# Attention of a two-layer hybrid transformer with expert retrieval: MLA heads one at a time in two of the six tiles

## The reference, cut to what matters

```python
def softmax_attend(q, k, v):                      # 8 MLA heads
    s = jnp.einsum('bqhd,bkhd->bhqk', q, k).astype(jnp.float32) * (q.shape[-1] ** -0.5)
    p = jax.nn.softmax(s, axis=-1)
    return jnp.einsum('bhqk,bkhd->bqhd', p.astype(v.dtype), v)

def diff_attend(q, k, v, lam):                    # 4 differential heads
    s = jnp.einsum('bqhcd,bkhcd->bhcqk', q, k).astype(jnp.float32) * (q.shape[-1] ** -0.5)
    p = jax.nn.softmax(s, axis=-1)
    a = p[:, :, 0] - lam * p[:, :, 1]
    return jnp.einsum('bhqk,bkhd->bqhd', a.astype(v.dtype), v)
```

## Time and profile before

| | us |
|---|---|
| median of 3 runs | 2632.14 (2626.13 to 2635.8) |
| the profiled execution | 2623.53 |
| its span | 2621.6 |
| TensorE busy | 2067.3 (79%) |
| VectorE busy | 1832.3 (70%) |
| ScalarE busy | 1119.5 (43%) |
| GpSimd busy | 975.2 (37%) |
| data moved | 980.25 MB, mean 374 GB/s |

### The profile page before, as it was taken

One profiled execution on the slowest core, in us unless ns is written; L12 is line 12 of the kernel. 1 busy time (PEld: TensorE's weight loads), 2 busy tenths in 40 slices (PEclk: granted clock), 3 DMA queues, 4 the chain that ended last, 5 costly groups with the idle time before them and its releaser, 6 DMA issues.

```text
span 2621.6 us, 26027 instructions
## 1 busy us (share of the span) xinstructions
PE 2067.3 (79%) x6888; PEld 1088.7 (42%) x6888; DVE 1832.3 (70%) x4176; ACT 1119.5 (43%) x3090; POOL 975.2 (37%) x916
## 2 busy tenths in 40 slices
PE   6997787777979876988677797878867988577766
PEld 2554444443435444444334343435543444333322
DVE  0147986995567779976979665644597787767776
ACT  2123474444236443744443723432244644333333
POOL 1012343332443433444343444320133443445453
PEclk8998898888998988989889898998988998888888
DMA  8588999997999999999999999994799999999997
GB/s 342 172 301 321 405 395 402 404 381 279 415 399 363 390 394 387 409 407 411 413 417 392 397 417 415 393 383 159 273 411 363 397 398 408 374 387 419 422 413 328
DMA packets 215704, 980.25 MB, mean 374 GB/s; under 512 B 17660, under 2 KB 75544, under 8 KB 117272
## 3 DMA queue, kind: packets, MB, share of 16 engines
q0 software_dynamic: 123648, 855.69, 80.1%
q1 hardware_dynamic: 91928, 123.05, 13.6%
HBM read 977.62 MB, written 1.05 MB: 373 GB/s over the span
## 4 chain that ended last, share of the span: by engine, by line
PE 32%; DVE 27%; DMA 22%; ACT 10%; issue 8%; POOL 1%; SPq 0%; POOLq 0%; DVEq 0%; ACTq 0%
DMA EXPERT<-in_peer_uv,FIX 19%; PE VS L1010 12%; PE PA L863 9%; DVE EXPERT L1630 9%; DVE ACC L1640 3%; DVE SCR L1264 2%; PE PA L891 2%; DMA WT<-in_peer_wq 2%; PE PB L787 2%; PE PB L1000 1%; PE VS L816 1%; ACT L1203 1%; PE PA L940 1%; PE PB L931 1%; ACT DIAG L1218 1%
## 5 line engine op out<-in xcount | busy, mean ns | idle before, releaser
L1010 PE MATMUL VS<-EXPERT,DIAG 128*128 128x512 f32 x2304 | 1170.4, 650 | 262.5 <-ACT DIAG L1218 261.8
L695 POOL DMA_INDIRECT EXPERT<-in_peer_uv,FIX x768 | 898.2, 1170 | 1088.4 <-PE VS L1010 739.1
L1630 DVE CUSTOM_DVE_ANT_0 EXPERT<-EXPERT,H 128x1024 f32<-128x1024 f32 x768 | 924.1, 1223 | 333.2 <-DMA EXPERT<-in_peer_uv,FIX 324.3
L1010 PEld LDWEIGHTS VS<-EXPERT,DIAG 128*128 128x128 f32 x2304 | 457.2, 209 | 840.9 <-issue 471.3
L1211 ACT ACTIVATE GEL<-DOT 128x1 f32<-128x1 f32 x768 | 155.2, 202 | 1046.6 <-DVE DOT L1630 1045.5
L863 PE MATMUL PA<-WT,HT 128*128 128x512 f32 (+2 forms) x720 | 294.5, 555 | 8.7 <-issue 5.4
L1640 DVE SCALAR_TENSOR_TENSOR ACC<-EXPERT,WEI,ACC 128x1024 f32<-128x1024 f32 x192 | 246.0, 1281 | 19.1 <-ACT WEI L1213 19.1
L1218 ACT ACTIVATE DIAG<-IDN,WEI 128x128 f32<-128x128 f32 x576 | 231.3, 402 | 60.0 <-PE VS L1010 41.9
L1000 PE MATMUL PB<-HT,WT 128*128 128x128 f32 (+1 forms) x1472 | 215.1, 308 | 35.1 <-issue 33.9
L1213 ACT ACTIVATE WEI<-GEL,GATE 128x1 f32<-128x1 f32 x768 | 226.3, 295 | 24.9
L1000 PEld LDWEIGHTS PB<-HT,WT 128*128 128x128 f32 x1472 | 207.8, 218 | 59.8 <-issue 57.2
(11 more groups left out here) (147 smaller groups left out, 1677.0 us busy)
## 6 DMA issues: line engine op xcount, KB each, us to landing
EXPERT<-in_w_ada POOLq DMA_DIRECT2D x48, 1024.0 KB, 11.9
WT<-in_peer_wq SPq DMA_DIRECT2D x92, 512.0 KB, 18.0
WT<-in_w_in SPq DMA_DIRECT2D x48, 512.0 KB, 10.0
WT<-in_w_out SPq DMA_DIRECT2D x48, 512.0 KB, 9.9
EXPERT<-in_peer_uv,FIX POOLq DMA_INDIRECT x768, 11.4
WT<-in_w_in SPq DMA_DIRECT2D x16, 384.0 KB, 9.8
WT<-in_w_in SPq DMA_DIRECT2D x16, 288.0 KB, 6.6
WT<-in_mla_wq_up SPq DMA_DIRECT2D x4, 512.0 KB, 10.0
```

Of the source, the lines that this page charges most:

```text
L695: pool.indirect_dma_start(out=EXPERT[:, j, :], out_offset=None, in_=a["peer_uv"], in_offset=bass.IndirectOffsetOnAxis(ap=FIX[:, par, j:j + ...
L1010: ins = nc.tensor.matmul(VSUM[n][:, :], DIAG[:, i, :], EXPERT[:, j, D + n * W:D + (n + 1) * W], start=first, stop=last_one)
L1630: nc.vector.tensor_tensor_reduce(out=EXPERT[:, j, 0:D], in0=EXPERT[:, j, 0:D], in1=H2[:, b % HB, :], scale=1.0, scalar=0.0, op0=ALU.mult, ...
```

## The change

The pairs of heads were in all six tiles. The change adds a function `units` that gives each tile its list of units: in `(0, CTX, 0)` and `(1, LAT, 0)` eight single MLA heads and four differential heads, 12 units in stages -1 to 13; in the other four tiles the same 4 pairs and 4 differential heads as before. An attention stage costs the planner 35 in the two tiles and 50 in the others, as before. In the opening the new number of stages and their cost change where `mingle` puts the products. The stage `gates` (one VectorE instruction) is put after stage 9 instead of stage 3 in the pause.

```diff
+def units(l, g, t):
+    size = 1 if (l, g, t) in ((0, CTX, 0), (1, LAT, 0)) else 2
+    return [("mla", tuple(range(h, h + size))) for h in range(0, MH, size)] + [("diff", (h,)) for h in range(DH)]
...
 def cost(s):
+    if s[0] == "attn":
+        return 50 if len(units(*s[1:4])) < MH + DH else 35
...
-    keys, attend, leave = front(1, LAT, (1,), queries=False), gates_early(attention(1, LAT, 0), 5), outward(1, LAT, (0,))
+    keys, attend, leave = front(1, LAT, (1,), queries=False), gates_early(attention(1, LAT, 0), MH + 3), outward(1, LAT, (0,))
...
# TensorE
-                if i + 1 < UNITS:
-                    u = i + 1
-                    for c in range(2):
+                todo = units(l, g, t)
+                if i + 1 < len(todo):
+                    kind, hs = todo[i + 1]
+                    for c in range(2 if kind == "diff" else len(hs)):
                         bank = fill_b()
...
-                    for c in range(2 if u < PAIRS else 1):
+                    for c in range(len(hs)):
                         bank = fill_a()
-                        turn_tiles(bank, [PR[:, u % 2, c, k * P:(k + 1) * P] for k in range(keys // P)], P)\
+                        turn_tiles(bank, [PR[:, (i - 1) % 2, c, k * P:(k + 1) * P] for k in range(keys // P)], P)\
...
# VectorE
-                    if done < PAIRS:
-                        tt(o.rearrange("p (c n) -> p c n", c=2), bank[:, 0:P].rearrange("p (c n) -> p c n", c=2),
-                           INV[:, done % 2, :].unsqueeze(2).to_broadcast([P, 2, MD]), ALU.mult).then_inc(emptied_a, 1)
+                    if done == "mla":
+                        tt(O[:, hs[0] * MD:hs[0] * MD + n].rearrange("p (c n) -> p c n", c=len(hs)),
+                           bank[:, 0:n].rearrange("p (c n) -> p c n", c=len(hs)),
+                           INV[:, i % 2, 0:len(hs)].unsqueeze(2).to_broadcast([P, len(hs), MD]), ALU.mult)\
+                            .then_inc(emptied_a, 1)
```

More of the change, by code:

```diff
@@ L106, in front @@
     return out
+def units(l, g, t):
+    size = 1 if (l, g, t) in ((0, CTX, 0), (1, LAT, 0)) else 2
+    return [("mla", tuple(range(h, h + size))) for h in range(0, MH, size)] + [("diff", (h,)) for h in range(DH)]
 def attention(l, g, t):
-    out = [("attn", l, g, t, i) for i in range(-1, UNITS + 2)]
+    out = [("attn", l, g, t, i) for i in range(-1, len(units(l, g, t)) + 2)]
     return out + [("gates", l, g, t), ("hnorm", l, g, t), ("rows", l, g, t, 0), ("heads", l, g, t), ("rows", l, g, t, 1)]
@@ L326, in make_plan @@
     plan += keys[:1] + g1 + [("adae", 1, 2)] + keys[1:at] + sh2[:2] + [("adat", 1, 2)] + keys[at:]
[L327 removed]
+    at = attend.index(("attn", 1, LAT, 0, MH + DH - 2)) + 1
     plan += attend[:at] + [sh2[2], attend[at], sh2[3], ("adae", 1, 3), attend[at + 1], sc2[0], attend[at + 2], ("adat", 1, 3)]
@@ L921, in attn @@
                     pe.wait_ge(emptied_a, ra.n)
-                if i + 1 < UNITS:
-                    u = i + 1
-                    for c in range(2):
+                todo = units(l, g, t)
+                if i + 1 < len(todo):
+                    kind, hs = todo[i + 1]
+                    for c in range(2 if kind == "diff" else len(hs)):
                         bank = fill_b()
-                        if u < PAIRS:
-                            q, k = QTM[:, 2 * u + c, t * P:(t + 1) * P], KTM[:, 2 * u + c, 0:keys]
-                        else:
-                            q = QTD[64 * c:64 * c + 64, u - PAIRS, t * P:(t + 1) * P]
-                            k = KTD[64 * c:64 * c + 64, u - PAIRS, 0:keys]
+                        if kind == "mla":
+                            q, k = QTM[:, hs[c], t * P:(t + 1) * P], KTM[:, hs[c], 0:keys]
+                        else:
+                            q = QTD[64 * c:64 * c + 64, hs[0], t * P:(t + 1) * P]
+                            k = KTD[64 * c:64 * c + 64, hs[0], 0:keys]
@@ L939, in attn @@
+                    for c, h in enumerate(hs):
                         for k in range(keys // P):
-                            last = nc.tensor.matmul(bank[:, c * MD:c * MD + n], PT[:, c, k * P:(k + 1) * P], v[:, k, at:at + n],
-                                                    start=(k == 0), stop=(k == keys // P - 1))
+                            last = nc.tensor.matmul(bank[:, c * n:(c + 1) * n], PT[:, c, k * P:(k + 1) * P],
+                                                    v[:, k, h * n:(h + 1) * n], start=(k == 0), stop=(k == keys // P - 1))
@@ L942, in attn @@
                     last.then_inc(filled_a, 1)
-                if 1 <= i <= UNITS:
-                    u = i - 1
-                    if u < PAIRS:
+                if 1 <= i <= len(todo):
+                    kind, hs = todo[i - 1]
+                    if kind == "mla":
                         pe.wait_ge(exp_ready, tick.so_far("units") + 1)
@@ L1151, in attn @@
                 keys = 2 * P if g == CTX else 4 * P
-                u = i + 1
+                u, todo = i + 1, units(l, g, t)
                 if u == 0 and t == 0 and l == g:
                     table_of(ACT.Exp)
-                if u < UNITS:
+                if u < len(todo):
+                    kind, hs = todo[u]
                     act.wait_ge(negmax_ready, tick("negmax"))
-                    for c in range(2):
+                    for c in range(2 if kind == "diff" else len(hs)):
                         bank = from_b()
                         ins = nc.scalar.activation(PR[:, u % 2, c, 0:keys], bank[:, 0:keys], ACT.Exp,
-                                                   bias=NM[:, u % 2, c:c + 1], scale=SC_M if u < PAIRS else SC_D,
+                                                   bias=NM[:, u % 2, c:c + 1], scale=SC_M if kind == "mla" else SC_D,
                                                    accum_out=SUM[:, u % 2, c:c + 1])
@@ L1459, in attn @@
                 keys = 2 * P if g == CTX else 4 * P
-                u = i + 1
-                if u < UNITS:
-                    for c in range(2):
+                u, todo = i + 1, units(l, g, t)
+                if u < len(todo):
+                    kind, hs = todo[u]
+                    maps = 2 if kind == "diff" else len(hs)
+                    for c in range(maps):
                         bank, n = rb.next()
@@ L1468, in attn @@
                 if i >= 2:
-                    done = i - 2
+                    done, hs = todo[i - 2]
                     bank = from_a()
-                    o = O[:, done * P:(done + 1) * P]
-                    if done < PAIRS:
-                        tt(o.rearrange("p (c n) -> p c n", c=2), bank[:, 0:P].rearrange("p (c n) -> p c n", c=2),
-                           INV[:, done % 2, :].unsqueeze(2).to_broadcast([P, 2, MD]), ALU.mult).then_inc(emptied_a, 1)
-                    else:
-                        nc.vector.tensor_copy(o, bank[:, 0:P]).then_inc(emptied_a, 1)
@@ L1477, in attn @@
-                if 1 <= i <= UNITS:
-                    for c in range(2 if i - 1 < PAIRS else 1):
+                    n = len(hs) * MD
+                    if done == "mla":
[3 more added lines that the diff above has]
+                            .then_inc(emptied_a, 1)
+                    else:
+                        at = MH * MD + hs[0] * P
+                        nc.vector.tensor_copy(O[:, at:at + P], bank[:, 0:P]).then_inc(emptied_a, 1)
@@ L1479, in attn @@
+                if 1 <= i <= len(todo):
+                    for c in range(len(todo[i - 1][1])):
                         bank = from_a()
                         nc.vector.tensor_copy(PT[:, c, 0:keys], bank[:, 0:keys]).then_inc(emptied_a, 1)
-                if u < UNITS:
+                if u < len(todo):
                     dve.wait_ge(dve_step, steps[0])
-                    nc.vector.tensor_scalar(NM[:, u % 2, :], MX[:, u % 2, :], -(SC_M if u < PAIRS else SC_D), None,
+                    nc.vector.tensor_scalar(NM[:, u % 2, 0:maps], MX[:, u % 2, 0:maps], -(SC_M if kind == "mla" else SC_D), None,
@@ L1484, in attn @@
                                             ALU.mult).then_inc(negmax_ready, 1)
-                if 0 <= i < UNITS:
+                if 0 <= i < len(todo):
+                    kind, hs = todo[i]
+                    maps = 2 if kind == "diff" else len(hs)
                     dve.wait_ge(exp_ready, tick("exp"))
                     dve.wait_ge(emptied_a, ra.n)
-                    link(nc.vector.reciprocal(INV[:, i % 2, :], SUM[:, i % 2, :]))
-                    if i >= PAIRS:
+                    link(nc.vector.reciprocal(INV[:, i % 2, 0:maps], SUM[:, i % 2, 0:maps]))
+                    if kind == "diff":
```

8 lines of the change are left out of this document (2 added, 6 removed).

## The result

| | us |
|---|---|
| median before | 2630.67 (5 runs, 2626.13 to 2635.8) |
| median with the change | 2616.1 (5 runs, 2603.73 to 2619.78) |
| ratio | 0.9948, 95% interval 0.9926 to 0.997 |
| the profiled execution | 2613.29, span 2611.3 |

14.6 us less, where 2.3 were forecast; the time lies just under the range. The page of the profile: busy times within 4 us of those before (weight loads 8.5 less), 24 VectorE instructions more.

A forecast was written before the change was run, and what follows sets the result against it. TensorE was taken as the bound in the opening's and the pause's attention, with gains only in its idle and slow time. Pause -2.9 and opening +0.6 gave -2.3 us, so 2632.1 became 2629.8 us; range 2617 to 2639.

The forecast's parts named there:

- The slow clock: Pause, 1811 to 1827 us: mean clock 0.62, about 12 us at 1.2 GHz; the forecast sum counted no gain from it.
- the other case: Rival that the slow clock goes too: pause gains 2.9 + 6 us, opening up to 3 more; chance 0.27.
- The long wait of the opening: TensorE's 2.45 us wait at the opening's first turn, right before clock 0.61 over 8 us; removed, with 2.5 at the second.
- Its size: Loss to the slow clock in the pause: half of about 12 us at 1.2 GHz, 6 us.
- the rival on the slow clock: Slow clock goes in the pause and perhaps the opening: kernel at 2620.8 to 2624 us; chance 0.27.
- Waits removed, start, more steps: Pause's attention: -4.0 us of waits, +0.35 at the start, +0.8 for steps; sum -2.9, ends -4.3 to -0.9.
- more steps: Pause: four more TensorE steps, 0.2 us each for switches between kinds of matmuls, +0.8 us (0 to 1.6).
- VectorE keeps up: Pause: TensorE stays the bound of a 2.46 us step by a tenth of a microsecond; extra small VectorE instructions cost nothing.
- The opening: Opening's attention: -2.45 us at the first turn, +2.5 at the second, +0.6 for steps; sum +0.6, from -2.4 to +2.
- Faster by over 0.5%: Whole kernel: both slow stretches gone and all waits with them, -13 us; chance 0.06.

The follow-up runs named there:

- run 4: Kernel before (pairs), with an idle 128x256 product ahead of each of the six waiting scores of the pause: 2617.96 us, ratio 0.9955 to before.
- run 9: Changed kernel, plus second scores of the pause's differential heads behind the transposes and the opening's second turn a stage later: 2613.55 us, ratio 0.996 to before.
- run 5: Changed kernel, with the pause's scores of heads 3, 5 and 7 made to wait for the preceding head's exponential: 2629.68 us, ratio 1.0011 to before.
- Run 10: Kernel of run 5, with two idle 128x256 products ahead of each of the three waits put back: 2620.14 us, ratio 0.9983 to before.
- run 3: Kernel before (pairs), with each unit's second score in the pause behind the transposes and its maximum behind the copies: 2608.34 us, ratio 0.9932 to before.
- run 6: Kernel of run 3, with the first turn of the opening one attention stage later: 2605.44 us, ratio 0.9918 to before.
- run 8: Changed kernel measured again, nothing altered, on another chip than the first follow-ups: 2615.67 us, ratio 0.9969 to before.
- run 1: Kernel before, with single heads in the pause tile alone and pairs kept in the opening: 2610.89 us, ratio 0.994 to before.
- run 12: Kernel before, unchanged, traced a second time: pause's attention 55.2 us at mean clock 0.72; no median given.

## Why the prediction was wrong

- *The slow clock*. This is the step that failed. The forecast left the 12 us at 1.2 GHz of the pause where they were and gave the other case 0.27. They hung on the waits: with these filled (run 4), and with most of them taken away by single heads (three traces) or late scores (four), the stretch ran at 1.00 throughout (run 9, which has both, fell for 3.4 us), with three waits put back (run 5) at 0.62. Run 10, filled in part, lies between. The rows had hinted at it: the fall came after 24 us with 5 us of idle time. I held against it that no row shows how small a gap is small enough, which is a reason for doubt about the size, not for leaving the clock as it was. What makes the clock fall at one gap and not at another stays open (1.47 us in run 3 without a fall, 0.86 in run 9 with one). The long wait of the opening, which the prediction set beside this one, is at least not needed for the slow stretch there: run 6 took it away and the stretch stayed, behind a wait of 0.68 us.
- *Its size*. The prediction priced it at 6 us from one execution; against run 4's 44.1 us, pairs at full clock, that execution gives 49.3 - 44.1 = 5.2, the other two traces 55.2 - 44.1 = 11.1. With the mean of the three (53.2) the pause gives 53.2 - 39.7 = 13.5 us; the medians gave 14.6, 17 and, in run 8, 7. The range ended at 2617 since it rested on the mildest execution, and the rival on the slow clock, 2620.8 at best with the opening's stretch in it, fell short of the measured 2616.1 too, though only the pause's stretch went.
- *Waits removed, start, more steps* (-2.9 us). The direction and the places were right; the size was 4.4: run 4, pairs at full clock with their waits, takes 44.1 us, and single heads 39.7. The term mis-sized is "more steps", +0.8: the step came out at 2.39 us and not 2.46, and half of a pair's step without its wait is 2.35 (from 1796.04 to 1801.86 us before, less 1.13), so the switches between kinds of matmuls cost next to nothing over what the pairs paid. The prediction left two waits, 0.55 and 0.61 us; three of 0.62 stand there. The third, at the last differential head, did not show before because the clock was slow there; run 4 has it too.
- *VectorE keeps up.* Right, with the small margin that was counted. The small instructions do cost VectorE time (busy 30.1 us instead of 28.8 in the stretch, for 12 more instructions) and cost the tile next to none, as the sum said.
- *The opening* (+0.6). Right, as far as it can be told: +0.5 in the mean of five executions each, with a spread of up to 3 us, and the wait moved to the second turn.
- *Faster by over 0.5%* got 0.06, and only with both slow stretches and all waits gone. One stretch and most of the waits of the pause were enough for 0.5% (0.6% in run 1, 0.3% in run 8). It should have been several times that.

## What to carry to other kernels

A short wait of TensorE can cost twice: its own length, and what its work loses if the clock falls for it. Here 4 to 5 us of waits, none over 1.13 us, brought 5 to 11 us more. Where a stretch at 1.2 GHz follows a row of gaps, count it as likely that it goes with them, but test it: in the opening it stayed when the long gap went. Trace more than one execution, since the length of such a stretch varies. Before splitting the work into smaller units, try to move the instruction that waits behind others that don't: that took all but one of these waits away from full-sized pairs, and though the transposes then waited 3.0 us for VectorE, the pause took 38.0 us in four traces, less than with single heads (39.6 to 39.8).

## What the runs showed of the hardware

The clock fell though no gap was longer than 1.13 us (pairs in the pause, three traces), and 1.4 us after the end of one of 1.89 us (run 5); it stayed up behind one of 1.47 us (run 3). Once at 1.2 GHz the array can stay there without being idle at all: in run 12, from 1809 to 1838 us, TensorE runs one matmul after another (scores of 64 rows, value products of 64 and 128 columns, transposes), busy for 29.00 of 29 us, and the mean granted clock is 0.50; 8 transposes take 1.91 us there instead of 1.04. TensorE: Matmul & The Clock Gate (The HAM clock gate) of the Trainium skill has activity release the throttle; this stretch was busy throughout and yet stayed slow for 29 us, so the trace does not agree with it as it stands. An idle product of 0.60 to 0.70 us in each of the first six gaps kept the full clock through the pause (run 4, one trace).
